# A hybrid attention and recurrence layer on one core: x's mean and root a body sooner, other orders on ScalarE and VectorE

## The chip, the core and the metric

The kernel runs on one core of a Trainium2 chip. Five engines of that core work side by side, each through its own list of instructions in its own order: TensorE (matrix products and transposes; PE in the profile, PEld for its weight loads), VectorE (DVE), ScalarE (ACT), GpSimd (POOL), and SyncE (SP), which here issues transfers. They meet only at semaphores. An engine whose next instruction waits for a semaphore stands still, and so does all that is queued behind that instruction on the same engine. The metric is the device time of one execution in microseconds (us). Each kernel is timed in several executions, and one execution is recorded by the hardware profiler.

## What is computed

```python
h = rmsnorm(x, ln_gain)                       # x: 2048 tokens x 1024
z = h @ w_in                                  # 1024 x 4608
q, k, v, g_attn, x_lru, g_lru = split(z)
# group A: 16 query heads on 4 key/value heads of 64, window of 128 tokens,
#          rotary on the first 16 dimensions, one learned sink per head
s = where(in_window, (q @ k.T) / 8, -1e30)
m = maximum(max(s), sink)
p = exp(s - m) / (sum(exp(s - m)) + exp(sink - m))
y_a = rmsnorm((p @ v) * silu(g_attn), gain_a)
# group B: causal convolution of width 4, then a gated linear recurrence
u = conv(x_lru) + b
r, i = sigmoid(u @ W_r + b_r), sigmoid(u @ W_i + b_i)     # blocks of 64
a = exp(-8 * r * softplus(-lam))
h_t = a_t * h_(t-1) + sqrt(1 - a_t**2) * (i_t * u_t)
y_b = rmsnorm(h * silu(g_lru), gain_b)
out = rmsnorm(x + concat(y_a, y_b) @ w_out, final_gain)
```

Products are kept near float32 precision: each factor is split into a high part (rounded to float32r) and a low part (what the rounding left), and TensorE adds three products, high x high, high x low and low x high.

## The kernel before, in words

There are two phases. Phase A makes the projections, the attention and the recurrence, and writes both groups' results to memory. Phase B multiplies them with w_out, adds x and normalises. The change is in phase A.

Phase A goes through 16 **bodies**: four quarters of 512 tokens (`q` 0 to 3), and in each the four groups of channels (`g` 0 to 3). `n` counts bodies from 0 to 15; -1 is the work before the first. A body projects nine weight tiles of 128 columns, in TensorE's order XL0, XL1, GL0 (recurrent input and its gate), GA0, GA1 (attention gate), GL1, and then for the next body KVG, Q0 and Q1. A project is 8 x 3 = 24 products of 128x512 into one bank of a ring of four. The rest of TensorE's list is put between the projects:

XL0, XL1, GL0, gates(0), score(0), score(1), gates(1), GA0, score(2), GA1, turn_p(0), score(3), turn_x, GL1, weigh_v(0), turn_p(1), KVG, weigh_v(1), turn_p(2), Q0, weigh_v(2), turn_p(3), Q1, weigh_v(3), turn_v.

`score(b)` makes the scores of **tile** b, the b-th block of 128 tokens; it writes over tile b-2's bank (for b=3 over tile 2's, so it waits until VectorE's `select(2)` has read that). `turn_p(b)` transposes the tile's weights (after `softmax_b(b)`), `weigh_v(b)` multiplies them with v (after `low_p(b)`). `gates(u)` are the two gates of the recurrent **unit** u (two units of 128 channels a body); it waits for `low_u(u)`.

**x for the next quarter.** In the twelve bodies of the quarters 0 to 2, `turn_x` transposes one block of 128 tokens of x, after it was normalised in place. The steps are: SyncE loads the block (`load_x`, L553); ScalarE squares and sums it (`square_x`, L725) in the body before; VectorE makes the mean (`stat_x`, L1054), ScalarE the root (`root_x`, L730), VectorE the reciprocal (L1059) and the scaling (`norm_x`, L1061); TensorE turns it (L1585); ScalarE and VectorE write high and low part (`high_x` L735, `low_x` L1067).

**Weights.** In the first quarter (`split` true, n = 0 to 3) the weights come as float32: ScalarE rounds a tile to its high part (`split_w`, L718, 128x1024), VectorE takes the low part (L1046), and SyncE writes both back to memory (L509). In n = 0 to 2 (`split_next`) the tiles for the next body are split too. Later quarters load both parts back. There are three slots; tile i uses slot i mod 3, and a split into a slot waits until its last content has been written to memory (`kept_before`, L717).

**Each tile of the softmax.** ScalarE copies the scores (`s_copy(b)`, L850), VectorE puts in the scores of the block before (`select(b)`, L1235) and takes the maximum (`top(b)`, L1251), ScalarE makes the exponentials (`s_exp(b)`, four ACTIVATEs at L858), VectorE the reciprocal and the product (`softmax_b(b)`, L1256 and L1259), TensorE turns (`turn_p`, L1548), ScalarE writes the high part (`high_p(b)`, L866), VectorE the low part (`low_p(b)`, L1264), GpSimd masks both (L643), TensorE multiplies (`weigh_v`, L1561), ScalarE and VectorE take the result (`low_o` L871, `add_o` L1273, `gate_o` L1281).

**Each unit of the recurrence.** ScalarE takes the input (`lru_in`, L880 to L891), VectorE convolves (`conv`, three at L1298, of which the first waits for L885), ScalarE and VectorE split the result (`high_u` L896, `low_u` L1304), TensorE makes the gates, ScalarE reads them (`take_gates`, four 64x512 ACTIVATEs at L913 and L915), then `first_decay` (L923), `decays` (L929, L935), VectorE `one_less` (L1318) and `input_x` (L1323), ScalarE the root (`lru_root`, L939), VectorE `lru_tail` (L1329), `lru_scan` (L1341, L1344) and `silu_l` (L1309). `gate_a` (L844) and `gate_l` (L901) are ScalarE's tanh of the gates, `silu_a` (L1218) VectorE's product with them.

ScalarE evaluates a root with another table than exp and tanh, so each change between them stands as an ACT_TABLE_LOAD in its list.

All orders are written out by hand in the function `body` of each engine; nothing is rearranged by a planner.

## Time and profile before

| | |
|---|---|
| time, median of 3 executions | 1451.74 us (1450.38 to 1453.25) |
| the profiled execution's own time | 1450.79 us |
| span of the profile | 1449.2 us |
| PE busy | 1381.1 us, 95% of the span |
| PEld busy | 1126.7 us, 78% |
| DVE busy | 974.6 us, 67% |
| ACT busy | 818.9 us, 57% |
| POOL busy | 203.2 us, 14% |
| mean granted TensorE clock | 0.976 of full speed |
| DMA queue of SP | 217.79 MB, 44.5% of the 16 engines' span |

The span runs from the first to the last instruction; 1.6 us of the execution's time lie around it. Busy time is the time in which an engine had at least one instruction at work. A matmul's row shows its whole passage (0.39 us for 512 columns) while the next starts 0.23 us later, so that rates are read from starts. The granted clock is 1.0 at 2.4 GHz and 0.5 at 1.2 GHz. In phase A a body of the first quarter takes about 71 us, one of the second and third 66 to 67 us, one of the last 62 to 64 us.

### The profile page before, as it was taken

Reading aid. Unit: us, or ns where it says so; the run is one execution under the profiler, and the core shown is the slowest. Engines: PE = TensorE matmul, PEld = TensorE weight load, DVE = VectorE, ACT = ScalarE, POOL = GpSimd, SP = SyncE. Lnnn points to the kernel's source line nnn. Section 1 sums busy time; section 2 is a strip of 40 time slices with the busy share of each in tenths; the row PEclk is TensorE's granted clock in tenths of the full one; section 3 lists DMA queues with packets and bytes.
Section 4 is the critical chain, followed back from the end, with each engine's and each line's share of the span. In section 5 each row is a group of like instructions: output and inputs, shape, how many; then the busy total and the mean of one; then the engine's idle time right before and its main releaser. Section 6 shows DMA issues by size and latency. Waiting matters only on the chain.

```text
span 1449.2 us, 22243 instructions
## 1 busy us (share of the span) xinstructions
PE 1381.1 (95%) x6756; PEld 1126.7 (78%) x6756; DVE 974.6 (67%) x1663; ACT 818.9 (57%) x1695; POOL 203.2 (14%) x251
## 2 busy tenths in 40 slices
PE   9898989899999999999999999999998999999998
PEld 7686868687878787787878787777777888888886
DVE  6787878777676768676776767776876644343442
ACT  7867676747475666747474756758484322222120
POOL 2030303021111112020212112030211000000000
PEclk9998999999999999999999999999999999999999
DMA  9675757653545464544535474545536332232320
GB/s 335 212 250 188 250 193 245 218 201 137 200 147 183 141 210 145 194 149 159 193 133 203 148 262 149 190 161 188 196 103 222 113 116 88 86 116 72 101 87 29
DMA packets 98289, 243.22 MB, mean 168 GB/s; under 512 B 8112, under 2 KB 43056, under 8 KB 98224
## 3 DMA queue, kind: packets, MB, share of 16 engines
q1 hardware_dynamic: 91200, 217.79, 44.5%
q0 software_dynamic: 7024, 24.65, 4.5%
q8 instruction: 31, 0.51, 0.1%
q14 instruction: 34, 0.28, 0.1%
HBM read 179.49 MB, written 62.91 MB: 167 GB/s over the span
## 4 chain that ended last, share of the span: by engine, by line
PE 66%; ACT 15%; DVE 9%; issue 7%; DMA 1%; POOL 1%; ACTq 1%; DVEq 0%; SPq 0%; POOLq 0%
PE ring L1498 35%; PE acc_b L204 12%; PE ring L204 11%; PE ps_tv L1561 3%; ACT p_sb L858 3%; ACT ri L915 2%; ACT ra L929 2%; ACT ra L913 2%; ACT s_sb L850 1%; PE ring L1585 1%; ACT hs L923 1%; PE ps_tv L1548 1%; DVE w_lo L1046 1%; PE ring L1575 1%; DVE rows L1061 1%
## 5 line engine op out<-in xcount | busy, mean ns | idle before, releaser
L1498 PE MATMUL ring<-split,w_hi 128*128 128x512 f32 x2288 | 731.5, 401 | 8.0 <-DVE w_lo L1046 8.0
L1498 PEld LDWEIGHTS ring<-split,w_hi 128*128 128x128 f32 x2288 | 431.3, 193 | 104.4 <-ACT cu L885 7.7
L1498 PE MATMUL ring<-split,w_lo 128*128 128x512 f32 x1144 | 453.3, 396 | 0.0
L1498 PEld LDWEIGHTS ring<-split,w_lo 128*128 128x128 f32 x1144 | 218.9, 191 | 47.4
L643 POOL TENSOR_SCALAR_AFFINE_SELECT p_hi_c<-p_hi 128x512 fp32r<-128x512 f32 x64 | 44.3, 693 | 747.0 <-ACT p_hi L866 747.0
L858 ACT ACTIVATE p_sb<-s_sb,smax 128x129 f32<-128x129 f32 x256 | 99.3, 392 | 0.2
L1298 DVE SCALAR_TENSOR_TENSOR cu<-xl,prm,cu 128x512 f32<-128x512 f32 x96 | 72.0, 750 | 31.3 <-ACT cu L885 26.4
L1788 ACT ACTIVATE w_hi<-res 128x1024 fp32r<-128x1024 f32 x15 | 15.9, 1059 | 134.4 <-DVE res L1858 134.4
L204 PE MATMUL acc_b<-wo_rest,y_own 128*128 128x512 f32 x384 | 89.8, 390 | 1.8 <-DVE wo_rest L165 1.8
L204 PE MATMUL ring<-split,y_own 128*128 128x512 f32 x384 | 91.2, 392 | 0.0
L204 PEld LDWEIGHTS acc_b<-wo_rest,y_own 128*128 128x128 f32 x384 | 71.9, 188 | 17.2 <-DVE wo_rest L165 2.3
L204 PEld LDWEIGHTS ring<-split,y_own 128*128 128x128 f32 x384 | 71.4, 188 | 14.8
L1858 DVE SCALAR_TENSOR_TENSOR res<-acc_b,rms,res 128x1024 f32<-128x1024 f32 x15 | 19.3, 1285 | 80.2 <-PE acc_b L204 80.1
L204 PE MATMUL acc_b<-wo_rest,w_hi 128*128 128x512 f32 x256 | 69.7, 389 | 0.0
L204 PE MATMUL ring<-split,w_hi 128*128 128x512 f32 x256 | 69.6, 394 | 0.0
L1264 DVE TENSOR_TENSOR p_lo<-ps_tv,p_hi 128x512 fp32r<-128x512 f32 x64 | 44.2, 690 | 33.4 <-ACT p_hi L866 32.4
L1281 DVE TENSOR_TENSOR ya<-ya,o_sb 128x256 f32<-128x256 f32 x64 | 63.0, 984 | 1.6
L643 POOL TENSOR_SCALAR_AFFINE_SELECT p_lo_c<-p_lo 128x512 fp32r<-128x512 f32 x64 | 55.1, 861 | 33.1 <-DVE p_lo L1264 31.2
L1235 DVE COPY_PREDICATED s_sb<-prev_mask,ps_s 128x512 f32<-128x512 uint8 x48 | 35.4, 737 | 35.4 <-ACT s_sb L850 35.4
L1273 DVE TENSOR_TENSOR o_sb<-ps_tv,kc_ol 64x256 f32<-64x256 f32 x128 | 53.4, 418 | 6.6 <-ACT kc_ol L871 2.8
L901 ACT ACTIVATE gl<-ring 128x512 f32<-128x512 f32 x32 | 19.2, 599 | 65.9 <-PE ring L1498 58.3
L204 PEld LDWEIGHTS acc_b<-wo_rest,w_hi 128*128 128x128 f32 x256 | 48.0, 188 | 10.0
(246 smaller groups left out, 2370.3 us busy)
## 6 DMA issues: line engine op xcount, KB each, us to landing
w_hi<-w_split_scratch SPq DMA_DIRECT2D x108, 512.0 KB, 3.3
w_lo<-w_split_scratch SPq DMA_DIRECT2D x108, 512.0 KB, 4.4
w_raw<-w_tiles_d SPq DMA_DIRECT2D x36, 512.0 KB, 4.4
w_split_scratch<-w_hi SPq DMA_DIRECT2D x36, 512.0 KB, 5.1
w_split_scratch<-w_lo SPq DMA_DIRECT2D x36, 512.0 KB, 5.9
y_scratch<-hs POOLq DMA_DIRECT2D x32, 256.0 KB, 4.5
y_scratch<-ya POOLq DMA_DIRECT2D x16, 512.0 KB, 6.6
rows<-y_scratch SPq DMA_DIRECT2D x8, 1024.0 KB, 7.8
```

The costliest lines, as they stand in the source:

```text
L204: last = self.nc.tensor.matmul(banks[:, ACC[s, g][h], :], y[s][:, e, :], self.wo(e, low)[:, h * (D // 2):(h + 1) * (D // 2)], start=(e % ( ...
L643: nc.gpsimd.affine_select(out=dst[:, :, :], in_=f(src[:, :, :]), compare_op=ALU.is_ge, fill=0.0, base=0, pattern=[[0, GQ], [1, BLK]], chan ...
L858: nc.scalar.activation(p_sb[:, b % 2, h, :], s_sb[:, b % 2, h, :], ACT.Exp, bias=smax[:, b % 2, 0, h:h + 1], accum_out=sden[:, b % 2, 0, h ...
L913: nc.scalar.activation(ra[u][to, :], bank(r)[to, :], ACT.Tanh, scale=0.5, bias=prm[to, C_BR, bass.ds(G, 1)]).then_inc(*gate_r.one())
L915: nc.scalar.activation(ri[u][to, :], bank(r)[rows, :], ACT.Tanh, scale=0.5, bias=prm[to, C_BI, bass.ds(G, 1)]).then_inc(*ring_act.one())
L1235: nc.vector.copy_predicated(s, prev_mask[:, :, :], scores_of(b)[:, :, 0:BLK]).then_inc(*s_sel.one())
L1264: nc.vector.tensor_tensor(p_lo[:, :, :], ps_t[:, :, :], f(p_hi[:, :, :]), ALU.subtract).then_inc(*p_low.one())
L1273: nc.vector.tensor_tensor(o_sb[s * HD:(s + 1) * HD, :, :], pair(ps_v[0:HD], s), pair(o_low, s), ALU.add).then_inc(*o_sum.one())
L1281: nc.vector.tensor_tensor(y, y, o_sb[:, :, :], ALU.mult).then_inc(*ya_done.one())
L1298: stt(out=cu[u][:, :], in0=xl[:, tap:tap + T], scalar=prm[:, C_W0 + tap, bass.ds(G, 1)], in1=cu[u][:, :], op0=ALU.mult, op1=ALU.add).then_ ...
L1498: last = mm(bank(r), w[:, i % WSLOTS, k, :], h[:, par, k, :], start=(k == 0 and j == 0), stop=(k == KC - 1 and j == 2))
L1561: last = mm(ps_v[:, :, :], v[:, b, :], p[:, :, :], start=(i == 0), stop=(i == 3))
```

## The change

Nothing is computed otherwise; instructions move, and two small ones per body are added.

- **x.** `root_x(n)` and its mean `stat_x(n)` now follow `square_x(n)` in the same body n, for the block that body n+1 normalises: the mean on VectorE after `low_q(n, 0)`, the root at the very end of ScalarE's body. Behind the root stands `exp_table()`, an exp of one column into a scratch column, which brings the other table back. `norm_x` moves up on VectorE from behind `softmax_b(1)` to in front of `select(0)`. For n = -1 square and root stand in the start of the program, while the root's table is still in place.
- **ScalarE's order.** `s_copy(2)` comes right after `s_exp(0)`, then `take_gates(1)` (before: ahead of `decays(0)`), `gate_a(0)`, `s_exp(1)` and only then the second unit's decays; `high_p(0)` and `gate_a(1)` come ahead of the roots; `s_copy(3)` and `s_exp(2)` behind `high_x`.
- **VectorE's order** follows: `select(2)` after `softmax_b(0)`, `input_x(1)`, `one_less(1)`, `low_p(0)` after `softmax_b(1)`, and `select(3)`, `top(3)`, `softmax_b(2)` behind `low_x`.
- **Weights.** In the first quarter the split of GL0 (the third tile) stands in front of `lru_in(0)` on ScalarE and of `conv(0)` on VectorE.
- The signals of mean and root start one body ahead (`ahead=1`), since the start of the program now makes them once.

```diff
@@ root of x, ScalarE
-            def root_x(n, xms, xroot):
-                act.wait_ge(*xms)
-                nc.scalar.activation(xs[:, 2:3], xs[:, 1:2], ACT.Sqrt).then_inc(*xroot.one())
+            def root_x(n):
+                act.wait_ge(*x_ms.at(n, 1))
+                act.wait_ge(*x_rs.at(n, 1))
+                nc.scalar.activation(xs[:, 2:3], xs[:, 1:2], ACT.Sqrt).then_inc(*x_root.one())
+
+            def exp_table():
+                nc.scalar.activation(table_sink[:, :], ones[:, :], ACT.Exp).then_inc(x_early_root, 1)
@@ start of the program, ScalarE
             split_w(-1, Q1)
+            square_x(-1)
+            root_x(-1)
...
             high_v(-1)
-            square_x(-1)
@@ one body, ScalarE
+                if split:
+                    split_w(n, GL0)
                 lru_in(0)
                 high_q(n - 1, 1)
...
                 if split:
-                    split_w(n, GL0)
                     split_w(n, GA0)
...
                 first_decay(0)
-                take_gates(1)
                 decays(0)
                 if split:
                     split_w(n, GL1)
                 s_exp(0)
+                s_copy(2)
+                take_gates(1)
+                gate_a(0)
+                s_exp(1)
                 first_decay(1)
                 decays(1)
-                gate_a(0)
-                s_copy(2)
-                s_exp(1)
-                if q < NQUART - 1:
-                    root_x(n, x_ms.at(n, 1), x_root)
+                high_p(0)
+                gate_a(1)
                 lru_root(0)
                 lru_root(1)
                 if split_next:
                     split_w(n, KVG)
-                s_exp(2)
-                high_p(0)
-                gate_a(1)
-                s_copy(3)
                 if q < NQUART - 1:
                     for half in range(2):
                         high_x(h_hi[:, 1 - par], g * P, half, bank(R_XT0 + half),
                                ring_ready.at(n, R_XT0 + half + 1), h_high.one())
                 elif g > 1:
                     proj.high_w(act, 2 * g - 3)
+                s_copy(3)
+                s_exp(2)
...
                     high_v(n)
+                if x_follows(q, nxt_par != par):
+
+                    root_x(n)
+                    exp_table()
@@ mean of x, VectorE
-            def stat_x(sq_in, xms):
-                dve.wait_ge(*sq_in)
+            def stat_x(n):
+                dve.wait_ge(*x_sq.at(n, 1))
+                dve.wait_ge(*x_root.at(n, 0))
                 nc.vector.tensor_scalar(xs[:, 1:2], xs[:, 0:1], 1.0 / D, EPS, ALU.mult, ALU.add
-                                        ).then_inc(*xms.one())
+                                        ).then_inc(*x_ms.one())
@@ norm_x now waits for the root that the body before made
+            def norm_x(n):
+                dve.wait_ge(*x_root.at(n, 0))
...
@@ one body, VectorE
                 sink_in()
+                if split:
+                    split_w(n, GL0)
                 conv(0)
                 low_gates()
                 low_u(0)
-                if split:
-                    split_w(n, GL0)
-                if q < NQUART - 1:
-                    stat_x(x_sq.at(n, 0), x_ms)
...
                 low_v(n, g)
+                if q < NQUART - 1:
+                    norm_x(n)
                 select(0)
                 top(0)
                 select(1)
                 top(1)
                 input_x(0)
-                one_less(0)
                 if split:
                     split_w(n, GL1)
+                one_less(0)
                 softmax_b(0)
-                input_x(1)
-                silu_a(0)
-                one_less(1)
                 select(2)
                 top(2)
+                silu_a(0)
                 softmax_b(1)
-                if q < NQUART - 1:
-                    norm_x(n, x_root.at(n, 1), x_rs, x_norm)
+                input_x(1)
+                one_less(1)
+                low_p(0)
+                silu_a(1)
                 lru_tail(0)
                 lru_scan(0)
                 if split_next:
                     split_w(n, KVG)
-                low_p(0)
-                softmax_b(2)
-                silu_a(1)
-                select(3)
-                top(3)
...
                     proj.low_w(dve, 2 * g - 3)
+                select(3)
+                top(3)
+                softmax_b(2)
...
                     add_q(n, 0)
                     low_q(n, 0)
+                if x_follows(q, nxt_par != par):
+                    stat_x(n)
+                if not last:
                     turn_q(n, 1)
                     add_q(n, 1)
```

On ScalarE, in a body of the first quarter: the exponentials of tile 0 (`s_exp(0)`) and what follows them. Before:

```order
L858 ACTIVATE p_sb,sden<-s_sb,smax 128x129 x4
L920 REGISTER_ALU
L923 ISA
L923 ACTIVATE hs<-ra,prm 128x512
L928 REGISTER_ALU
L929 ISA
L929 ACTIVATE ra<-ra,prm 128x512
L931 REGISTER_ALU
L935 ACTIVATE a<-ra 128x512
L841 REGISTER_ALU
L844 ACTIVATE ya<-ring 128x512
```

And now, from the same exponentials on (of the four ACTIVATEs of `take_gates(1)`, `ra` and `ri`, all but the last two stand here):

```order
L864 ACTIVATE p_sb,sden<-s_sb,smax 128x129 x4
L854 REGISTER_ALU
L855 REGISTER_ALU
L856 ACTIVATE s_sb<-ps_s 128x4x128
L915 REGISTER_ALU
L919 ISA
L919 ACTIVATE ra<-ring,prm 64x512
L921 ISA
L921 ACTIVATE ri<-ring,prm 64x512
```

The copy of tile 2's scores (`s_sb<-ps_s`) had the second unit's decays and `gate_a(0)` between itself and tile 0's exponentials, and has nothing there now. The decays come after tile 1's exponentials.

On ScalarE, at the end of a body in the loop over g: the split of v, and how the loop goes on. Before:

```order
L804 ACTIVATE vraw<-v_carry 128x64
L810 ACTIVATE v_hl<-vraw 128x5x64
L472 REGISTER_ALU
L472 COMPARE_AND_BRANCH
L880 ACTIVATE xl<-x_carry 128x3
```

And now (`x_stat` is the root of x's mean, `w_hi` the split of GL0, `xl` the first instruction of `lru_in(0)`):

```order
L811 ACTIVATE vraw<-v_carry 128x64
L817 ACTIVATE v_hl<-vraw 128x5x64
L732 ACT_TABLE_LOAD
L732 ACTIVATE x_stat<-x_stat 128x1
L735 ACT_TABLE_LOAD
L735 ACTIVATE table_sink<-ones 128x1
L473 REGISTER_ALU
L473 COMPARE_AND_BRANCH
L719 ACTIVATE w_hi<-w_raw 128x1024
L886 ACTIVATE xl<-x_carry 128x3
```

Two table loads and two small ACTIVATEs have come between a body's last instruction and the next body's first, and in the first quarter the split of GL0 as well.

On VectorE, between tile 1's softmax and the first unit's tail (`hs` in `ri<-ri,hs`). Before:

```order
L1259 TENSOR_TENSOR p_sb<-p_sb,sden 128x4x128
L1059 RECIPROCAL x_stat<-x_stat 128x1
L1061 SCALAR_TENSOR_TENSOR rows<-rows,x_stat 128x1024
L1329 TENSOR_TENSOR ri<-ri,hs 128x512
```

And now:

```order
L1271 TENSOR_TENSOR p_sb<-p_sb,sden 128x4x128
L1334 REGISTER_ALU
L1335 SCALAR_TENSOR_TENSOR ri<-ri,cu 128x512
L1329 REGISTER_ALU
L1330 SCALAR_TENSOR_TENSOR hs<-a,hs 128x512
L1276 TENSOR_TENSOR p_lo<-ps_tv,p_hi 128x512
L1230 SCALAR_TENSOR_TENSOR ya<-ya,ring 128x512
L1341 TENSOR_TENSOR ri<-ri,hs 128x512
```

The scaling of x (`rows<-rows,x_stat`) is gone from here to the place in front of `select(0)`; `input_x(1)`, `one_less(1)`, `low_p(0)` and `silu_a(1)` are what the first unit's tail stands behind now.

## Rows read from the trace of the kernel before

**Rows 1.** What TensorE waited for: engine, line, releaser: us in total, times, longest.

```profile
PE ring L1585 <- DVE rows L1061: 25.8, 12, 2.2
...
PE ps_s L1537 <- DVE s_sb L1235: 15.9, 16, 1.8
...
PE ring L1498 <- DVE w_lo L1046: 8.0, 4, 2.4
```

**Rows 2.** Timeline of TensorE, second body: start, duration, [idle before <-releaser].

```profile
114.18 0.72 PE L1498 MATMUL ring<-split,w_hi 128*128 128x512 f32 x2 [2.38 <-DVE w_lo L1046]
...
138.97 0.39 PE L1537 MATMUL ps_s<-k_hi,q_hi 64*128 64x256 f32 x2 [1.79 <-DVE s_sb L1235]
...
142.13 1.96 PE L1585 MATMUL ring<-ident,rows 128*128 128x128 f32 x8 [1.95 <-DVE rows L1061]
...
150.54 0.39 PE L1561 MATMUL ps_tv<-p_hi,v_hl 128*128 128x512 f32 x1
```

**Rows 3.** Timeline of TensorE, fifth body.

```profile
338.66 0.28 PE L1537 MATMUL ps_s<-k_hi,q_lo 64*128 64x256 f32 x2
...
345.89 0.39 PE L1537 MATMUL ps_s<-k_hi,q_hi 64*128 64x256 f32 x2 [0.85 <-DVE s_sb L1235]
...
349.06 1.96 PE L1585 MATMUL ring<-ident,rows 128*128 128x128 f32 x8 [2.19 <-DVE rows L1061]
...
358.06 0.39 PE L1561 MATMUL ps_tv<-p_hi,v_hl 128*128 128x512 f32 x1
...
359.33 0.71 PE L1498 MATMUL ring<-split,w_hi 128*128 128x512 f32 x2
...
364.91 0.39 PE L1561 MATMUL ps_tv<-p_hi,v_hl 128*128 128x512 f32 x1
```

**Rows 4.** A stretch of 10 us: TensorE's busy time, granted clock, DMA share.

```profile
346.00:356.00 10.00, 7.81 (x35) 0.66 0.25 97
```

**Rows 5.** Timeline of ScalarE, fifth body.

```profile
318.62 0.60 ACT L883 ACTIVATE xl<-ring 128x512 f32<-128x512 f32 x1 [3.27 <-PE ring L1498]
...
335.21 0.67 ACT L913 ACTIVATE ra<-ring,prm 64x512 f32<-64x512 f32 x1
...
338.03 0.82 ACT L929 ACTIVATE ra<-ra,prm 128x512 f32<-128x512 f32 x1
...
339.42 0.39 ACT L858 ACTIVATE p_sb<-s_sb,smax 128x129 f32<-128x129 f32 x1
...
340.96 0.80 ACT L923 ACTIVATE hs<-ra,prm 128x512 f32<-128x512 f32 x1
...
343.30 0.58 ACT L844 ACTIVATE ya<-ring 128x512 f32<-128x512 f32 x1
...
345.92 1.28 ACT L730 ACT_TABLE_LOAD   x1
...
348.47 1.28 ACT L858 ACT_TABLE_LOAD   x1
```

**Rows 6.** Timeline of VectorE, fifth body.

```profile
356.63 0.68 DVE L1329 TENSOR_TENSOR ri<-ri,hs 128x512 f32<-128x512 f32 x1
...
360.79 0.69 DVE L1264 TENSOR_TENSOR p_lo<-ps_tv,p_hi 128x512 fp32r<-128x512 f32 x1
```

**Rows 7.** Timelines of ScalarE, VectorE and SyncE, second body.

```profile
106.47 0.60 ACT L883 ACTIVATE xl<-ring 128x512 f32<-128x512 f32 x1 [0.88 <-PE ring L1498]
...
118.87 0.69 DVE L1304 TENSOR_TENSOR p_lo<-cu,p_hi 128x512 fp32r<-128x512 f32 x1 [0.70 <-ACT p_hi L896]
...
102.97 1.55 SPq L509 DMA_DIRECT2D w_split_scratch<-w_lo  x1
```

**Rows 8.** Transfers issued from 101 to 104 us, with KB and us to landing.

```profile
w_split_scratch<-w_lo SPq DMA_DIRECT2D x1, 512.0 KB, 5.7
```

**Rows 9.** Splits of the weights by line: xcount, busy, mean ns, idle before.

```profile
L1046 DVE TENSOR_TENSOR w_lo<-w_raw,w_hi 128x1024 fp32r<-128x1024 f32 x34 | 41.4, 1218 | 1.2 <-ACT w_hi L718 1.0
...
L718 ACT ACTIVATE w_hi<-w_raw 128x1024 fp32r<-128x1024 f32 x36 | 37.6, 1055 | 0.0
```

More of the change, by code:

```diff
@@ L373, in phase_a @@
         x_sq = signal("x_sq", 1, ahead=1)
-        x_ms = signal("x_ms", 1)
-        x_root = signal("x_root", 1)
+        x_ms = signal("x_ms", 1, ahead=1)
+        x_root = signal("x_root", 1, ahead=1)
         x_rs = signal("x_rs", 1)
@@ L740, in _ @@
             act.wait_ge(zeroed, 1)
-            nc.scalar.activation(xs[:, 2:3], ones[:, :], ACT.Sqrt).then_inc(x_early_root, 1)
+            nc.scalar.activation(table_sink[:, :], ones[:, :], ACT.Sqrt).then_inc(x_early_root, 1)
             for b in range(NBLK):
@@ L824, in _ @@
             nc.scalar.activation(prm[:, C_T2, :], prm[:, C_T0, :], ACT.Ln).then_inc(prm_act, 1)
-            nc.scalar.activation(xs[:, 2:3], ones[:, :], ACT.Exp).then_inc(x_early_root, 1)
+            exp_table()
             high_k(-1)
@@ L1050, in _ @@
                 dve.sem_inc(s.sem, s.prime)
-            def stat_x(sq_in, xms):
-                dve.wait_ge(*sq_in)
+            def stat_x(n):
+                dve.wait_ge(*x_sq.at(n, 1))
+                dve.wait_ge(*x_root.at(n, 0))
                 nc.vector.tensor_scalar(xs[:, 1:2], xs[:, 0:1], 1.0 / D, EPS, ALU.mult, ALU.add
-                                        ).then_inc(*xms.one())
-            def norm_x(n, root_in, xrs, xnorm):
-                dve.wait_ge(*root_in)
-                nc.vector.reciprocal(xs[:, 3:4], xs[:, 2:3]).then_inc(*xrs.one())
-                dve.wait_ge(*xrs.at(n, 1))
+                                        ).then_inc(*x_ms.one())
+            def norm_x(n):
+                dve.wait_ge(*x_root.at(n, 0))
+                nc.vector.reciprocal(xs[:, 3:4], xs[:, 2:3]).then_inc(*x_rs.one())
+                dve.wait_ge(*x_rs.at(n, 1))
                 stt(out=xb, in0=xb, scalar=xs[:, 3:4], in1=gain_row, op0=ALU.mult,
-                    op1=ALU.mult).then_inc(*xnorm.one())
+                    op1=ALU.mult).then_inc(*x_norm.one())
             def low_x(dst, hi, col, half, ps, ready, done):
@@ L1101, in _ @@
                     done(nc.vector.tensor_tensor(col(C_T0), col(C_LAM), col(C_T1), ALU.min))
+            stat_x(-1)
             def turn_k(n, g):
@@ L1350, in body @@
                 low_u(0)
-                if split:
-                    split_w(n, GL0)
-                if q < NQUART - 1:
-                    stat_x(x_sq.at(n, 0), x_ms)
-                elif g == 1:
+                if q == NQUART - 1 and g == 1:
                     proj.low_y(dve, 0, 0)
-                elif g > 1:
+                elif q == NQUART - 1 and g > 1:
                     proj.low_w(dve, 2 * g - 4)
```

2 lines of the change are left out of this document (added).

## The prediction

> **What bounds the kernel now.** I read first the busy shares, then TensorE's waits, then the granted clock, then three engines' timelines around the waits. TensorE is at work for 95% of the span; no other engine passes 67%. So what counts is TensorE's idle time and its clock, and everything else only as far as TensorE waits for it. Its waits in phase A have three places [rows 1]: `turn_x` waits 25.8 us for the scaled x (12 times), `score(3)` 15.9 us for `select(2)` (16 times), and the project of GL0 8.0 us for the low part of its weights (4 times, the first quarter). The timeline of one body of the first quarter has all three, 2.38, 1.79 and 1.95 us [rows 2]; one of the second quarter has the last two, 0.85 and 2.19 us [rows 3].
>
> The idle time has a second price. In the 10 us around the fifth body's `turn_x` the granted clock is 0.66 [rows 4]: part of the stretch ran at 1.2 GHz, the rest at 2.4. From `turn_x` to `weigh_v(0)` it took 9.00 us there and 8.41 in the second body [rows 2, 3]. At full clock a project takes 5.58 us (359.33 to 364.91), and four transposes 0.35 (weigh_v and turn_p together 1.27 from 358.06 to 359.33, four products of 0.23 off), so eight 0.7: in all 6.3. The fifth body lost 2.7 us, the second 2.1. Over the twelve bodies these spans sum to 101.1 us (7.96 to 9.07 each), which is 12 x 6.3 + 25. Two of the four GL0 projects, the second body's after 2.38 us of idle [rows 2] among them, took 1.6 us longer than the other two. So the three waits cost 25.8 + 15.9 + 8.0 = 49.7 in idle time and 25 + 3.2 in clock: **78 us**.
>
> **Part by part: what goes.** (1) *x a body sooner.* `norm_x` now waits for a root made a body ago, and stands before `select(0)`, over 12 us ahead of `turn_x`; its 1.4 us on VectorE fall where VectorE waits for tile 0's scores anyway (1.4 us idle before `select(0)` in the second body, more than 2 in the fifth). The 25.8 us go. (2) *Tile 2's scores.* `s_copy(2)` can start when TensorE has made them, 338.9 in the fifth body [rows 3]. Copy (0.5) and select (0.9) end at 340.5, while `score(3)` is wanted at 345.89 - 0.85 = 345.0: 15.9 us go, with 4.5 us to spare. (3) *GL0's split first*: 8.0 us go, if the split is not held up (below). With the idle time the 28 us of clock go.
>
> **What comes: ScalarE's two table loads at a body's end.** A load costs 1.28 us, and by the starts 1.3 (345.92 on) [rows 5]; two loads with their one-column ACTIVATEs 2.8 us, in eleven bodies. From the fifth body on they stand just before an idle of 3.27 us, in which ScalarE waits for the XL0 project [rows 5]: hidden, with 0.5 us to spare. The loads of the old place stay, since the units' roots stay there; only the 0.1 us root leaves.
>
> The Trainium skill, "ScalarE: Activation LUTs", section "What ACT_TABLE_LOAD costs", puts a switch at about 2.66 us, a 1283 ns load and 1380 ns of drain. The trace agrees with the load alone: the exp after the load at 348.47 starts 1.3 us after it. By the page the pair would be 5.4 us and would not fit the idle, and the sum would be some 30 us worse; I go by the trace.
>
> **What comes: the head of a body in the first quarter.** There ScalarE must split GL0 before `lru_in(0)`, and the split waits until the slot's last low part has been written: issued at 102.97, landed after 5.7 us [rows 7, 8], 108.7. The split (1.0) ends at 109.7, so `lru_in(0)` is 3.3 us later than at 106.47 [rows 7]. VectorE wins back 1.2 (GL0's low part [rows 9], which left its place behind `low_u(0)`), and some 0.8 that it idled. So `low_u(1)`, which ended at 119.56 [rows 7], ends 1.3 later, 120.9; TensorE without its GL0 wait (2.38) and slow clock (1.6) wants `gates(1)` at 119.7. A new wait of 1.2 us (bounds 0 and 3.3, the whole delay) in four bodies, and ScalarE's chain after it is 0.7 late against TensorE. GL0's own low part is there at 110.9, TensorE comes at 111.8.
>
> **What comes: tile 1.** With the stalls gone TensorE overtakes the softmax. It reaches `weigh_v(1)` in the fifth body at 364.91 - 0.85 - 2.19 - 2.7 = 359.2 [rows 3]. `low_p(1)` is at the end of this chain (starts from [rows 5]): without `take_gates(1)` (335.21 to 338.03, 2.82) `s_exp(0)` starts at 336.6 and ends at 338.1; `s_copy(2)` waits for 338.9 and ends at 339.5; `take_gates(1)` 342.3; `gate_a(0)` 0.5, `s_exp(1)` 1.6: 344.4; the second unit's decays 2.34 (340.96 to 343.30): 346.8; `high_p(0)`, `gate_a(1)` 0.5 each: 347.8; load and both roots 2.45 (345.92 to 348.47 less the old root): 350.2; `high_x` and `s_copy(3)` 1.5: 351.7; load 1.3: 353.0; `s_exp(2)` 1.6: 354.6. On VectorE `softmax_b(2)` 0.8, then from the second unit's tail to the end of `low_p(1)` 4.5 (356.63 to 361.48, less 0.3 idle [rows 6]): 359.9. So TensorE waits **0.7 us**. The step sizes are sure to 0.1 but a dozen are added: bounds 0 and 2.
>
> In bodies 0 to 2 the splits of KVG (ScalarE 1.0) and Q0 (VectorE 1.2) [rows 9] stand inside that chain, GL1's split lets tile 0's exponentials end 0.4 us after tile 2's scores are there, which adds 0.4, the late head 0.7: 0.7 + 1.0 + 1.2 + 0.4 + 0.7 = **4.0 us** (bounds 2.5 and 5.5). After an idle of 2.38 the clock fell; after these it will, for 1.6 to 2.7 us: 2.0. Idles of 0.65 us stand in the last four bodies and no slow clock follows them, so 0.7 us should cost no clock.
>
> **The rest.** The last quarter has no x; its four 0.65 us waits at `score(3)` go (in the 15.9 above), and its tile 1 gets 0.35 us later against TensorE: 1.4. At the start, `square_x(-1)` and its root now stand in ScalarE's way before the rotary work; its block of x lands late there, and ScalarE is 3 us behind; TensorE had less than 2 us in hand for XL0's split: 1.2 (bounds 0 and 3).
>
> **The sum.** Gone 78. Come: bodies 0 to 2, 3 x (4.0 + 2.0 + 1.2) = 21.6; body 3, 0.7 + 0.7 + 1.2 = 2.6; eight bodies 8 x 0.7 = 5.6; last quarter 1.4; start 1.2: 32.4. Net -45.6 from the profiled execution's 1450.8 (span 1449.2 and 1.6 around it): 1405. The median of the three runs is 0.9 higher, so the forecast is **1406 us**.
>
> **Rivals.** *Tile 1 longer, and the clock with it.* If the chain is 1.3 us longer than I add, TensorE idles 2 us at `weigh_v(1)` in nine bodies; an idle of 1.79 was followed by slow clock in the second body, one of 1.78 in the third only after the next wait. Price 9 x (1.3 + 1.7) = 27: **1433**. For it: the chain has a dozen links, each with a start delay. Against: the longest chain that I can build gives 1.2.
>
> *Less given back.* If the first-quarter chain has slack (the GL1 split fits in a gap, the keep lands early), 4.0 becomes 2.5 and `gates(1)` waits nothing: -(3 x 1.5 + 4 x 1.2) = -9, and the eight 0.7 vanish, -6: **1391**.
>
> *The waits stay, by another releaser.* That the change does not do what it says would be `turn_x` waiting for its bank, or `score(3)` for a select held up behind `softmax_b(0)`. The 4.5 us of room speak against it; half of the 78 kept: **1445**.
>
> *Slower than before.* One mechanism could do it: ScalarE's queue. `s_exp(2)` stands behind two table switches, and if a switch held the queue for twice what its row shows, tile 2's softmax, the second unit's scan and `low_p(1)` would all come 2.6 us later, the head of each body 2.2 us late as well (2.8 doubled less 3.3 idle), and the slow clock would stay. In twelve bodies 2.6 + 2.2 + 2.7 on top of 32: 90 + 32 against 78: **1496**. It decides from 78 / 12 = 6.5 us given back per body; my sum has 2.7. The rows of the loads speak against it.
>
> **How the numbers follow.** Forecast 0.74, its own range 1396 to 1417; tile 1 longer 0.10; less given back 0.09; waits stay 0.04; slower 0.03. The range of 8 in 10 takes part of both neighbours: 1393 to 1423. Under 0.2% (3 us) a difference can't be told from none: faster 0.96, same 0.01, slower 0.03.
>
> **What would show it.** In the profile after: no row of TensorE waiting for `rows` or for `s_sb`'s select; GL0 gone from the waits; instead waits of about 4 us at `weigh_v(1)` for `low_p` in three bodies and under 1 in the others, waits of 1 us at `gates` in four; ACT busy up by 11 x 2.8 = 31 us with no new wait behind it from the fifth body on; bodies of the middle quarters near 62.5 us; mean clock up from 0.976 to about 0.99. Wrong it would be if slow clock still stood in the middle quarters, or if TensorE waited for `xl` or the gates there.

## The result, and the profile after

The changed kernel took 1412.21 us (median of four runs, 1411.69 to 1414.68) beside 1451.06 for the kernel before: ratio 0.9735, 95% interval 0.9717 to 0.9753. A second set of runs on another occasion gave 1412.01, ratio 0.9752 (0.9736 to 0.9768). The forecast of 1406 (1393 to 1423) had the sign and the size; it is 6 us too low.

The page's line of busy times, after:

```profile
PE 1366.1 (97%) x6756; PEld 1111.4 (79%) x6756; DVE 975.5 (69%) x1663; ACT 850.7 (60%) x1728; POOL 206.5 (15%) x251
```

The span is 1410.9 us, 38.3 shorter. TensorE's idle time (span less busy) went from 68.1 to 44.8, its busy time from 1381.1 to 1366.1 with the same 6756 matmuls: 23.3 us of idle and 15.0 us of clock. The mean granted clock rose from 0.976 to 0.991. ScalarE is 31.8 us busier.

What TensorE waited for, after (engine, line, releaser: us in total, times, longest):

```profile
PE ps_tv L1574 <- DVE p_lo L1276: 25.7, 16, 3.4
PE ring L1588 <- DVE gl L1321: 3.5, 3, 1.4
...
PE ring L1511 <- DVE w_lo L1055: 0.6, 3, 0.2
```

Of [rows 1] two rows are gone: in phase A nobody waits for the scaled x (`rows`) or for `select(2)` any more, and 0.6 is left of GL0's 8.0. In their place stands one large row, `weigh_v` waiting for the low part of the softmax weights (2.6 us in 6 waits before), and three waits at `gates`, 3.5 in all. The timeline of TensorE in the fifth body answers to [rows 3]:

```profile
332.25 0.39 PE L1550 MATMUL ps_s<-k_hi,q_hi 64*128 64x256 f32 x2
...
333.15 1.09 PE L1598 MATMUL ring<-ident,rows 128*128 128x128 f32 x8
334.00 0.71 PE L1511 MATMUL ring<-split,w_hi 128*128 128x512 f32 x2
...
339.55 0.39 PE L1574 MATMUL ps_tv<-p_hi,v_hl 128*128 128x512 f32 x1
...
346.17 0.39 PE L1511 MATMUL ring<-split,w_lo 128*128 128x512 f32 x1
348.20 0.50 PE L1574 MATMUL ps_tv<-p_hi,v_hl 128*128 128x512 f32 x1 [1.65 <-DVE p_lo L1276]
```

`score(3)` (332.25) and `turn_x` (333.15) start without idle time. From `turn_x` to `weigh_v(0)` it is 6.4 us, where [rows 3] had 9.00. The new wait stands at `weigh_v(1)`. The granted clock of three stretches. Each line gives the stretch and its length, the busy time of TensorE, of its weight loads, VectorE, ScalarE and GpSimd, then the clock, the DMA share and GB/s; the last two lie around a wait at `weigh_v(1)`:

```profile
82.00:86.00 4.00, 3.68 (x12) 3.02 (x13) 3.97 (x9) 1.23 (x3) 0.93 (x1) 0.58 0.52 208
...
346.00:356.00 10.00, 8.22 (x38) 6.22 (x37) 9.00 (x17) 3.57 (x6) 3.76 (x4) 1.00 0.31 108
664.00:674.00 10.00, 9.55 (x36) 7.54 (x37) 8.02 (x15) 4.23 (x7) 3.45 (x4) 0.83 0.26 100
```

Around the end of the 3.4 us waits in the first three bodies the clock falls to 1.2 GHz for a while (0.58 from 82 to 86 us); behind the 1.65 us wait at 348.20 it stays at 2.4 GHz (1.00), behind the same wait at 664.32 it does not (0.83). ScalarE's timeline at the head of the fifth body:

```profile
302.92 1.28 ACT L732 ACT_TABLE_LOAD   x1
304.21 0.20 ACT L732 ACTIVATE x_stat<-x_stat 128x1 f32<-128x1 f32 x1
304.43 1.28 ACT L735 ACT_TABLE_LOAD   x1
305.73 0.20 ACT L735 ACTIVATE table_sink<-ones 128x1 f32<-128x1 f32 x1
305.84 0.19 ACT L886 ACTIVATE xl<-x_carry 128x3 f32 x1
```

The two loads and their ACTIVATEs take 2.9 us, and `lru_in(0)` follows at once: the 3.27 us idle of [rows 5] is used up, with nothing of it to spare.

The second body has a late head, as forecast, but not for the reason forecast; one row of each engine's timeline (TensorE, ScalarE, VectorE):

```profile
119.02 0.49 PE L1588 MATMUL ring<-p_hi,gw_hi 64*128 64x512 f32 x2 [1.34 <-DVE gl L1321]
```

```profile
106.22 1.04 ACT L719 ACTIVATE w_hi<-w_raw 128x1024 fp32r<-128x1024 f32 x1
107.17 0.19 ACT L886 ACTIVATE xl<-x_carry 128x3 f32 x1
```

```profile
117.68 0.69 DVE L1316 TENSOR_TENSOR p_lo<-cu,p_hi 128x512 fp32r<-128x512 f32 x1 [0.70 <-ACT p_hi L902]
118.29 0.68 DVE L1321 SCALAR_TENSOR_TENSOR gl<-gl,ring 128x512 f32<-128x512 f32 x1
```

GL0's split (106.22) stands ahead of `lru_in(0)` (107.17). It starts without idle time right behind the two table loads, and in the kernel without these loads (below) it starts at 104.39. So here it is the loads that hold the split, while the forecast let it wait for its slot in memory and gave the loads no cost in the first quarter. `low_u(1)` ends at 118.37, but `gates(1)` waits until 119.02, for the ring bank that `silu_l(0)` (118.29 and 0.68) reads.

### The profile page after: what moved, and what is told of

It reads as the page before. It is cut to its first block, busy times and chain, and to the rows that moved or that the text cites. A ratio compares the mean times of both kernels' runs of the same rounds, so it can differ in the third digit from the quotient of the medians.

```text
span 1410.9 us, 22300 instructions
## 1 busy us (share of the span) xinstructions
PE 1366.1 (97%) x6756; PEld 1111.4 (79%) x6756; DVE 975.5 (69%) x1663; ACT 850.7 (60%) x1728; POOL 206.5 (15%) x251
## 4 chain that ended last, share of the span: by engine, by line
PE 60%; ACT 15%; DVE 11%; issue 9%; DMA 2%; POOL 1%; ACTq 1%; DVEq 1%; POOLq 0%; SPq 0%
PE ring L1511 30%; PE acc_b L204 11%; PE ring L204 11%; ACT p_sb L864 3%; PE ps_tv L1574 2%; DVE hs L1353 2%; ACT ri L921 2%; PE ring L1588 1%; ACT ra L919 1%; PE ps_s L1550 1%; DVE ri L1341 1%; ACT ra L935 1%; ACT hs L929 1%; ACT ya L850 1%; PE ps_tv L1561 1%
## 5 line engine op out<-in xcount | busy, mean ns | idle before, releaser
L1511 PE MATMUL ring<-split,w_hi 128*128 128x512 f32 x2288 | 720.0, 396 | 0.6 <-DVE w_lo L1055 0.6
L1511 PEld LDWEIGHTS ring<-split,w_hi 128*128 128x128 f32 x2288 | 423.9, 189 | 93.2 <-issue 4.5
L1511 PE MATMUL ring<-split,w_lo 128*128 128x512 f32 x1144 | 447.3, 391 | 0.0
L1511 PEld LDWEIGHTS ring<-split,w_lo 128*128 128x128 f32 x1144 | 215.7, 189 | 46.1
L644 POOL TENSOR_SCALAR_AFFINE_SELECT p_hi_c<-p_hi 128x512 fp32r<-128x512 f32 x64 | 50.6, 791 | 626.0 <-ACT p_hi L872 626.0
L1801 ACT ACTIVATE w_hi<-res 128x1024 fp32r<-128x1024 f32 x15 | 15.9, 1060 | 134.4 <-DVE res L1871 134.4
L204 PE MATMUL ring<-split,w_hi 128*128 128x512 f32 x256 | 70.0, 395 | 0.0
L877 ACT ACTIVATE kc_ol<-ps_tv 64x512 f32<-64x512 f32 x64 | 38.0, 593 | 46.5 <-PE ps_tv L1574 45.3
L1293 DVE TENSOR_TENSOR ya<-ya,o_sb 128x256 f32<-128x256 f32 x64 | 63.1, 986 | 1.6
L800 ACT ACTIVATE q_hi<-qrot 128x512 fp32r<-128x512 f32 x32 | 20.2, 630 | 59.0 <-DVE qrot L1161 59.0
L204 PEld LDWEIGHTS ring<-split,w_hi 128*128 128x128 f32 x256 | 47.8, 189 | 9.8
```

Of the source, the lines that this page charges most:

```text
L204: last = self.nc.tensor.matmul(banks[:, ACC[s, g][h], :], y[s][:, e, :], self.wo(e, low)[:, h * (D // 2):(h + 1) * (D // 2)], start=(e % ( ...
L644: nc.gpsimd.affine_select(out=dst[:, :, :], in_=f(src[:, :, :]), compare_op=ALU.is_ge, fill=0.0, base=0, pattern=[[0, GQ], [1, BLK]], chan ...
L877: nc.scalar.activation(o_low, ps_v[HD:, :, :], ACT.Copy).then_inc(*o_lowdone.one())
L1293: nc.vector.tensor_tensor(y, y, o_sb[:, :, :], ALU.mult).then_inc(*ya_done.one())
L1511: last = mm(bank(r), w[:, i % WSLOTS, k, :], h[:, par, k, :], start=(k == 0 and j == 0), stop=(k == KC - 1 and j == 2))
```

## The experiments

Each time is the median of four executions (five for x alone); the ratio is against runs of the kernel before on the same chip (median 1448.4 to 1449.1 beside the experiments), and where parts are compared, differences to those runs are used. "Idle" is span less TensorE's busy time. "Low clock" is the time at 1.2 GHz, which follows from the mean granted clock m as span x (1 - m) x 2; m is known to three digits, so it is good to about 1.5 us.

| kernel | us | ratio (95%) | idle | low clock |
|---|---|---|---|---|
| before | 1451.06 | 1 | 68.1 | 70 |
| changed | 1412.21 | 0.9735 (0.9717-0.9753) | 44.8 | 25 |
| GL0's split alone | 1438.75 | 0.9925 (0.9904-0.9947) | 58.9 | 66 |
| x alone | 1439.91 | 0.9928 (0.9898-0.9958) | 66.9 | 29 |
| order alone | 1466.03 | 1.0111 (1.0088-1.0134) | 87.1 | 94 |
| changed, without GL0 | 1427.66 | 0.9851 (0.9829-0.9873) | 52.7 | 40 |
| changed, without the order | 1424.84 | 0.9843 (0.9826-0.9859) | 55.3 | 20 |
| low_p(1) first | 1397.98 | 0.9651 (0.9635-0.9667) | 37.7 | 8 |
| low_p(1) first, gate earlier | 1397.01 | 0.9644 (0.9628-0.9660) | 36.0 | 8 |
| Q0's low part behind | 1413.61 | 0.9755 (0.9738-0.9771) | 44.7 | 28 |
| silu_l(1) first | 1407.11 | 0.9716 (0.9700-0.9732) | 44.9 | 11 |
| two more loads | 1435.37 | 0.9912 (0.9896-0.9929) | 56.2 | 34 |
| no loads at the body's end | 1412.55 | 0.9754 (0.9738-0.9770) | 45.2 | 25 |

### The three parts, each alone

**GL0's split alone.** The kernel before, on ScalarE and likewise on VectorE (there ahead of `conv(0)`):

```diff
+                if split:
+                    split_w(n, GL0)
                 lru_in(0)
 ...
-                    split_w(n, GL0)
                     split_w(n, GA0)
```

> The kernel before with GL0's split alone moved (ScalarE: ahead of lru_in(0); VectorE: ahead of conv(0)). Theory (the forecast's step 3): the 8.0 us of waits and 3.2 us of slow clock at GL0's project go, the late head is swallowed by the wait at turn_x that stays (about 26 us in 12 waits), score(3) still waits about 15: 1442 us, 1439 to 1446, 0.994 of before. Rival A (the late head of 3.3 us pushes turn_x's and the gates' waits in four bodies as far as it wins at GL0): no change, 1451. Rival B (GL0's wait is what makes the clock fall in the whole first quarter): 1430.

Measured 1438.75, 10.3 us under its runs of before. The other waits stay as they were:

```profile
PE ring L1586 <- DVE rows L1062: 26.0, 12, 2.2
PE ps_s L1538 <- DVE s_sb L1236: 15.8, 16, 1.8
```

GL0's row is gone, idle fell by 9.2 and busy by 3.2. The theory's mechanism holds: the waits at `turn_x` and `score(3)` stay as long as they were (26.0 against 25.8, 15.8 against 15.9). The time lies just under the range; as a difference it is -10.3 where the expectation had -9.

**x alone.** All of the change that concerns `square_x`, `stat_x`, `root_x`, `exp_table` and `norm_x`; nothing else.

> The kernel before with the x part alone (mean and root at a body's end, two table loads more there, norm_x ahead of select(0)); GL0's split and the order of scores, gates and decays as before. Theory (the three waits stand in a row, and what TensorE no longer waits at turn_x it waits further on, because tile 1's softmax, low_p(1) and score(3)'s select are late in the old order): turn_x's 25.8 us go, but about 20 us come at weigh_v(1) for low_p, GL0's grows from 8 to about 11, gates(1) 6, score(3) stays at about 14; total -4 in idle, and the clock still falls: 1443 us, 1436 to 1450. Rival A (each part takes away its own waits): 25.8 and some 15 of clock go: 1410. Rival B (the table loads are in the way): slower, 1465.

Measured 1439.91 (-9.2; the five executions spread from 1435.31 to 1443.86). Its waits:

```profile
PE ps_tv L1572 <- DVE p_lo L1274: 17.6, 18, 2.4
PE ps_s L1548 <- DVE s_sb L1245: 15.4, 16, 1.8
PE ring L1509 <- DVE w_lo L1053: 12.4, 5, 3.4
PE ring L1509 <- DVE split L1075: 5.6, 3, 1.9
```

The 25.8 us at `turn_x` are gone and 1.2 us of idle is won: TensorE now waits at `weigh_v(1)`, longer at GL0, and three times 1.9 us for the low part of x (`split`, L1075), in the last body of each of the first three quarters, where KVG is the first project that needs the new x. The 6 us that the expectation put at `gates(1)` did not come there. Nearly all of the gain is clock: busy time fell by 9.7 us. Almost the same idle total, spread otherwise, has 29 us of low clock instead of 70; why, no run here shows.

**The order alone.** The new order of scores, gates, decays and low parts, with x's mean, root and scaling in the same body as before (the root just ahead of `lru_root(0)`, `norm_x` ahead of `lru_tail(0)`).

> The kernel before with the order part alone (third scores' copy and select ahead of the second unit's decays, take_gates(1) behind them, tile 0's and 1's low parts ahead of the first unit's tail); x's mean, root and scaling in the same body as before (root just ahead of the units' roots, scaling ahead of lru_tail(0)). Theory (the order needs the x part: the root stands behind a longer row on ScalarE now): score(3) waits nothing, but turn_x waits 5 us in each of 12 bodies, 61 in all, against 25.8: slower, idle +18, clock +5: 1473 us, 1462 to 1480. Rival (parts are independent): score(3)'s 15.9 and 8 of clock go: 1427.

Measured 1466.03 (+16.9), slower, as the theory said. Its largest wait, and how it looks in a fifth body:

```profile
PE ring L1591 <- DVE rows L1065: 63.3, 12, 5.8
```

```profile
353.53 1.97 PE L1591 MATMUL ring<-ident,rows 128*128 128x128 f32 x8 [5.18 <-DVE rows L1065]
```

`score(3)`'s wait is gone, but the root that x's scaling needs now stands behind `take_gates(1)`, `s_exp(1)`, the decays and `high_p(0)` on ScalarE, so TensorE waits 5.18 us at `turn_x` where [rows 3] had 2.19. The loss is all idle time (19.0 us more); TensorE's busy time is 3.5 us lower than before, in spite of 94 us of low clock against 70, since part of the low clock now lies in the waits themselves (granted clock 0.82 from 348.35 to 353.50, with TensorE idle).

**Leaving one out.** The changed kernel with GL0's split back in its old place:

> The changed kernel with GL0's split put back in its old place on both engines (x part and order part stay). Theory: GL0's waits come back, larger than before (4 times 2.7, 10.9 us) since TensorE now arrives earlier, with slow clock behind them; weigh_v(1)'s waits of the first quarter shrink by less than 1 each: 1412 + 8 + 4 = 1424 us, 1419 to 1429. Rival (the late head that GL0's early split causes costs as much as it wins): 1412, no change.

And with the order undone (x and GL0 stay):

> The x part and GL0's split of the change, with the order of scores, gates and decays as before it: what the order part is worth when the others are there. Theory (the waits in a row: without the order, what turn_x no longer waits comes back at weigh_v(1), gates(1) and score(3)): about 20 us at weigh_v(1), 15 at score(3), 6 at gates(1); 1428 us, 1423 to 1434; the order part is then worth 16 us on top, though alone it cost 17. Rival (parts add up as measured one by one, -10.3 and -9.2): 1430 here, but then the order part would have to be worth -18 in the change and +17 alone; the waits tell: if turn_x's place shows no new waits but the gain is missing elsewhere, the theory is wrong.

Measured 1427.66 and 1424.84, both times inside the theory's ranges. The first:

```profile
PE ps_tv L1573 <- DVE p_lo L1275: 25.5, 16, 3.4
PE ring L1510 <- DVE w_lo L1054: 12.3, 7, 3.5
```

and the second:

```profile
PE ps_tv L1573 <- DVE p_lo L1275: 16.6, 17, 2.4
PE ps_s L1549 <- DVE s_sb L1246: 15.0, 16, 1.7
PE ring L1510 <- DVE split L1076: 5.6, 3, 1.9
```

In the second, `score(3)` waits as the theory said, `weigh_v(1)` 3 us less, and the last 6 us stand again at KVG, not at `gates(1)`.

Against the runs of before beside each kernel, the parts alone give -10.3, -9.2 and +16.9, in sum -2.6; together they give -36.4 to -38.9. With x in place the order is worth -12 (from x alone to the change without GL0; x alone is the least certain time here) and -13 with GL0 there too; without x it costs 17. GL0 is worth -10 alone, -14 with x in place, and -15 to -17 with x and the order: it is x that raises it, since TensorE then comes earlier and waits for GL0 10.6 us (of the 12.4 above) instead of 8.0. The waits stand in a row, and the removal of one is worth what the next leaves of it.

### The new wait

**low_p(1) first.** On VectorE, in every body but the last:

```diff
                 else:
-                    lru_scan(1)
-                    silu_l(1)
                     add_o(0)
                     low_p(1)
+                    lru_scan(1)
+                    silu_l(1)
```

> The changed kernel, with one edit on VectorE in every body but the last: add_o(0) and low_p(1) ahead of lru_scan(1) and silu_l(1) (3.1 us of work). Theory (weigh_v(1) waits because low_p(1) is at the end of VectorE's row, and the slow clock that is left follows these waits): the middle bodies' waits of 0.7 to 1.6 us at weigh_v(1) go, those of the first three bodies fall from 3.4 to about 1.2, the rest of the waits for p_lo is under 6 us; most slow clock outside the last quarter goes; 1412 - 14 (idle) - 5 (clock) = 1394 us, 1389 to 1400. Rival A (ScalarE's s_exp(2) is what is late, VectorE only follows): waits keep half their length, 1405. Rival B (the scan, now later, holds up the second unit's output and the next body): no gain, 1412.

Measured 1397.98, 14 us under the changed kernel. Its waits:

```profile
PE ps_tv L1574 <- DVE o_sb L1285: 12.8, 16, 2.1
PE ps_tv L1574 <- DVE p_lo L1276: 4.6, 4, 1.4
PE ring L1588 <- DVE gl L1321: 4.4, 4, 1.4
```

`p_lo` falls from 25.7 to 4.6. What comes is 0.8 us in `weigh_v(3)`'s wait for `add_o(1)`, which frees its bank, in eight bodies; no slow clock follows it between 222 and 1037 us. So it is VectorE's row, not ScalarE's `s_exp(2)` (rival A), that held `low_p(1)`, and the scan had room (rival B).

**The same, with gate_l(0) ahead of high_u(1) and silu_l(0) ahead of low_u(1).**

> The changed kernel with add_o(0) and low_p(1) ahead of lru_scan(1) and silu_l(1) on VectorE, and one edit for the waits at gates: ScalarE's gate_l(0) (the tanh) ahead of high_u(1), VectorE's silu_l(0) ahead of low_u(1). Theory (gates(1) waits in bodies 0 to 2 for the ring bank that silu_l(0)'s tanh empties): beyond the first edit alone, the 3 waits of 0.7 to 1.4 us go with the slow clock behind them: 1392 us, 1386 to 1398, about 2 under the first edit alone. Rival (low_u(1), now later, becomes the wait at gates(1) in its place): no difference from the first edit alone, or worse by up to 12 x 0.5.

Measured 1397.01. The waits at `gates` go from 4.4 to 2.4 us (now for `low_u(1)`: half theory, half rival); the two intervals overlap, so the gain of 1 us is not shown. Either of the two beats both kernels of this case.

**Q0's low part behind low_p(1)**, first quarter only, VectorE:

> The changed kernel, VectorE: the low part of Q0's split moved from ahead of lru_tail(1) to behind low_p(1), in the first quarter only. Theory (the first three waits at weigh_v(1) are longer than the others because the splits of the next weights stand in the chain, Q0's low part with 1.2): 3.4 falls to 2.3 in bodies 0 to 2, middle bodies unchanged; 1412 - 3 x 1.2 - some clock = 1408 us, 1404 to 1411. Rival (they are longer because the head is late by GL0): 3.4 stays, 1412.

Measured 1413.61. The waits fell as the theory said, the time did not. A first-quarter body of it:

```profile
151.26 0.50 PE L1574 MATMUL ps_tv<-p_hi,v_hl 128*128 128x512 f32 x1 [2.10 <-DVE p_lo L1276]
152.88 0.51 PE L1574 MATMUL ps_tv<-p_lo_c,dv_hl 128*128 128x512 f32 x1 [0.66 <-POOL p_lo_c L644]
```

3.4 became 2.1, and half of that is lost at the tile's last product, where TensorE now waits 0.66 us for GpSimd's copy of the low part. With 1.8 in place of 0.6 at `w_lo` the idle total is unchanged, 44.7. So Q0's split is part of the 3.4, but taking it out alone is worth nothing here; the expected 1404 to 1411 was missed.

### Why the middle bodies waited longer than forecast

The eight middle bodies wait 1.65, 1.17, 1.16, 0.69, 1.65, 1.65, 1.64 and 0.69 us at `weigh_v(1)`, 10.3 in all; 5.6 was forecast. VectorE and GpSimd in the fifth body (1.65):

```profile
343.99 1.76 DVE L1353 TENSOR_TENSOR_SCAN hs<-ra,h_carry,ri 128x512 f32<-128x512 f32 x1
...
347.45 0.69 DVE L1276 TENSOR_TENSOR p_lo<-ps_tv,p_hi 128x512 fp32r<-128x512 f32 x1
```

```profile
344.04 0.63 POOL L644 TENSOR_SCALAR_AFFINE_SELECT p_hi_c<-p_hi 128x512 fp32r<-128x512 f32 x1 [2.93 <-ACT p_hi L872]
```

and in the eighth (0.69):

```profile
533.35 1.28 DVE L1353 TENSOR_TENSOR_SCAN hs<-ra,h_carry,ri 128x512 f32<-128x512 f32 x1
...
536.34 0.69 DVE L1276 TENSOR_TENSOR p_lo<-ps_tv,p_hi 128x512 fp32r<-128x512 f32 x1
```

```profile
533.69 1.37 POOL L644 TENSOR_SCALAR_AFFINE_SELECT p_hi_c<-p_hi 128x512 fp32r<-128x512 f32 x1 [3.25 <-ACT p_hi L872]
```

Where the second unit's scan and GpSimd's copy of `p_hi` start within 0.05 us of each other, the scan takes 1.67 to 1.76 us instead of 1.28: at 344, 597, 660 and 725 us, the four bodies that wait 1.65. Where the scan is well ahead, it keeps its 1.28 and the copy takes 1.37.

The scan is half of the difference between 1.65 and 0.69. In the sixth and seventh bodies it keeps its 1.28 (at 407.58 and 470.71), and the wait is 1.17 and 1.16: 0.48 less than 1.65, and still 0.48 more than in the eighth. The sixth body, VectorE and TensorE:

```profile
407.58 1.28 DVE L1353 TENSOR_TENSOR_SCAN hs<-ra,h_carry,ri 128x512 f32<-128x512 f32 x1
```

```profile
411.32 0.50 PE L1574 MATMUL ps_tv<-p_hi,v_hl 128*128 128x512 f32 x1 [1.17 <-DVE p_lo L1276]
```

Of this second half 0.25 is VectorE, which is still at `top(3)` when `s_exp(2)` ends in the fifth and sixth bodies and is not in the eighth; the rest lies in ScalarE's row ahead of it.

The test of the scan's half: `silu_l(1)` ahead of the scan, so that the scan starts later against the copy.

```diff
-                    lru_scan(1)
                     silu_l(1)
+                    lru_scan(1)
                     add_o(0)
```

> The changed kernel; on VectorE, in every body but the last, silu_l(1) (0.7 us) ahead of lru_scan(1) instead of behind it: the same work, low_p(1) as far back as before. Theory (four of the middle bodies wait 1.65 us at weigh_v(1) instead of 0.7 to 1.2 because the second unit's scan there starts within 0.05 us of GpSimd's copy of p_hi, and takes 1.67 to 1.76 us instead of 1.28): the scan, 0.7 later, starts when that copy is over or nearly so; it takes 1.28 in the bodies that had 1.7 and at most 1.5 elsewhere, no middle body waits over 1.3, their waits sum to some 7 to 8 us instead of 10.3 and the slow stretch at 665 us goes: 1412 - 3 - 2 = 1407 us, 1404 to 1411. Rival (the waits differ because of what comes before, ScalarE's exponentials or x's low parts): the same pattern of 1.65 and 0.7, 1412.

Measured 1407.11, 4.9 us under the changed kernel on the same chip (1412.01), the intervals apart. VectorE in the body whose scan took 1.67 us in the changed kernel (at 596.57):

```profile
594.25 0.68 DVE L1321 SCALAR_TENSOR_TENSOR gl<-gl,ring 128x512 f32<-128x512 f32 x1
594.85 1.29 DVE L1353 TENSOR_TENSOR_SCAN hs<-ra,h_carry,ri 128x512 f32<-128x512 f32 x1
```

The eight waits are now all between 0.87 and 1.06 us (8.1 in all), and between 87 and 1046 us the clock never falls. The scans elsewhere went to 1.57 rather than the 1.5 at most that was expected. The expected time came, but not its split into 3 us of idle time and 2 of clock: all of the gain is clock. TensorE's busy time is 6.2 us lower than in the changed kernel's profile of the same occasion (1359.6 against 1365.8), and its idle time 1.7 higher (44.9 against 43.2), because waits elsewhere grew by more than the 2.7 us that `p_lo` lost (`o_sb` 3.6 against 0.7, `gates` 3.4 against 1.6).

### The table loads at a body's end

**Two more loads** behind the two (and two one-column ACTIVATEs), eleven bodies:

> The changed kernel with two more one-column ACTIVATEs (square root, exp; 2 more table loads, 2.8 us) behind the two at each body's end, eleven bodies. Theory (the first pair is hidden in ScalarE's wait for XL0, 3.3 us, with 0.5 to spare): this pair is hidden only in part; the head of the next body is 2.3 us late, conv and the gates swallow some of it, weigh_v(1) or gates wait longer: 1412 + 11 x (1 to 2.3) = 1430 us, 1423 to 1443. Rival A (ScalarE's queue has room all over): 1412 to 1416. Rival B (the first pair already costs its whole length): this one too, 1412 + 31 = 1443 with the waits in equal parts in all bodies.

**No loads there:** a copy in place of the root, and the one-column exp left out; this kernel leaves x's root out.

> The changed kernel with a copy in place of x's root at each body's end and without the one-column exp behind it, so without the 22 table loads there (leaves x's root out: x is scaled by the reciprocal of the mean square). Theory (they are hidden, as forecast): ScalarE's busy time falls by 31 us and the time by 0 to 3 us, from the gates' waits of bodies 1 to 3: 1410 us, 1408 to 1413. Rival (each load delays the next body's head in part, since ScalarE has only 0.5 us to spare): 11 x 1 us or more with the clock: 1400 or less.

Without the 22 loads: 1412.55, beside 1412.01 with them; ScalarE's busy time is 27 us lower (823.8 against 850.8; 31 was expected), `p_lo` 25.8 against 25.5. The loads cost the kernel nothing, as forecast. The split of GL0 in its second body, which is 0.9 us later there than in the changed kernel:

```profile
104.39 1.07 ACT L719 ACTIVATE w_hi<-w_raw 128x1024 fp32r<-128x1024 f32 x1
```

With 22 more: 1435.37, 23 us slower. Their trace at the head of the fifth body:

```profile
317.55 0.20 ACT L736 ACTIVATE table_sink<-ones 128x1 f32<-128x1 f32 x1
317.77 1.28 ACT L1044 ACT_TABLE_LOAD   x1
...
319.28 1.28 ACT L1045 ACT_TABLE_LOAD   x1
...
320.69 0.19 ACT L887 ACTIVATE xl<-x_carry 128x3 f32 x1
```

`lru_in(0)` is 3.0 us late there, and the waits at `gates` go from 3.5 us in three bodies to 12.8 in eleven. The first pair cost nothing, an equal second one 2.1 us a body, slow clock included (TensorE's busy time is 9.3 us above the changed kernel's, its idle time 11.4).

## Why the prediction was right, and where it was off

- **What goes.** All three waits went as written: `turn_x` 25.8, `score(3)` 15.9, GL0 8.0 but for 0.6. No releaser took the place of the old ones at these three places. This is the rival "the waits stay" ruled out.
- **Idle time.** Forecast net: 49.7 gone, 26.4 come, -23.3. Measured: 68.1 to 44.8, -23.3. That the two agree to 0.1 is luck, because errors cancel. The largest of them: the first three bodies wait 3.4 us at `weigh_v(1)`, not 4.0 (-1.8); `gates` waits in three bodies, 3.5 in all, not four times 1.2 (-1.3), and for `silu_l(0)`'s bank, one instruction behind the `low_u(1)` of the forecast; TensorE's first weight project at the start begins at 19.65 us instead of 19.61, so the 1.2 us there did not come (-1.2); the eight middle bodies wait 10.3, not 5.6 (+4.7).
- **The chain to low_p(1).** Checked in the fifth body: from `s_copy(2)` to the end of `s_exp(2)` 15.7 us were added up from single rows, and the trace has 15.8 (326.33 to 342.12); TensorE needs 20.2 us from there to `weigh_v(1)`, forecast 20.3. From the end of `s_exp(2)` to the end of `low_p(1)` the forecast has 5.3, the trace 6.0 (342.12 to 348.14); the first 0.25 of it is VectorE still at `top(3)`. This is where the terms were mis-sized. The scan was taken at the length it had in [rows 6]'s stretch, 1.28 within those 4.5 us, and took up to 0.48 more in four bodies, because the new order puts it beside GpSimd's copy: 1.9 of the 4.7 us. VectorE's `select(3)` and `top(3)`, which now stand ahead of `softmax_b(2)`, were put at nothing and held it up by 0.25, and some 0.2 came from the steps before, in all middle bodies but the last of a quarter (0.69, as forecast): the other 2.8. The silu-first kernel shows the scan's part, in which the 1.65 us waits became 1.05; the rest is read from rows and was not tested. The rows of ScalarE (start of `s_copy(2)`, last step of `s_exp(2)`):

```profile
326.33 0.60 ACT L856 ACTIVATE s_sb<-ps_s 128x512 f32<-128x512 f32 x1 [0.61 <-PE ps_s L1550]
...
341.93 0.19 ACT L864 ACTIVATION_READ_ACCUMULATOR p_sb<-s_sb,smax 128x1 f32 x1
```

- **The clock.** Here is the missing 7 us, and the step of the forecast that was off. It took 28 us off and gave 6 back, net 22; TensorE's busy time fell by 15.0. From before to low_p(1) first, 61 us less of low clock (70 to 8) came with 22.3 us less of busy time, 0.36 for one. By that price, an estimate, the 70 us of before cost 25, not 28, and the 25 us that are left cost 9, not 6. The price is not the same in every kernel (x alone 9.7 for 41, and the order alone runs the other way), since low clock in a wait costs nothing. What is left is more than forecast because the 1.65 us wait at 664.32 and the waits of 1.60 and 1.44 us in the last two bodies were followed by slow clock, and the forecast gave clock back in the first three bodies alone. The eight bodies' 0.7 "should cost no clock" was right of 0.7, but not of 1.65. So one sign by which the forecast named itself wrong did appear, slow clock in the middle quarters: 664 to 672 us in one execution, 408 to 416 and 600 to 608 in another. And most of the middle bodies take 63.1 us or more instead of 62.5.
- **The table loads.** They cost nothing, as shown by taking them out; but the 0.5 us to spare was not there, and in the second body they and not the slot delay the head. The price of 1.3 us from start to start was the right one: `lru_in(0)` starts 2.9 us after the first load. The Trainium skill, "ScalarE: Activation LUTs", section "What ACT_TABLE_LOAD costs", has about 2.66 us for a switch; by that a pair would have been some 5.3 us, an estimate that the trace contradicts.
- **Rivals.** "Tile 1 longer" (1433) was right on the mechanism: the wait is longer than forecast in six of the eight middle bodies, but by 0.5 to 0.95 instead of 1.3, and most of these waits kept the full clock. "Less given back" was right in part about the first quarter (3.4 at `weigh_v(1)`, not 2.5; `gates` 3.5 in all, not 0), wrong about the middle. The slower one needed loads that hold the queue twice as long as their rows show; no run has that.

## What to carry to other kernels

When several waits of one engine stand in a row, price them together: here three edits gave -10, -9 and +17 us alone and -36 to -39 as one. Before you count on an idle stretch as cover, work out how much of it is left afterwards: the first pair of table loads was free, the second cost 2.1 us for its 2.9. And when a sum of single rows puts an instruction in a new place, look at what the neighbour engine does at that moment: the scan was 0.15 to 0.48 longer beside a copy in seven bodies, and an order that moves it away from the copy is 4.9 us faster, all of it by the clock.
